# Eight experts in one loop with a question in each trip, or in one of two separate loops

## The reference, cut to what matters

```python
def moe_ffn(u, w_router, w13, w2):
    t = u.reshape(-1, D)
    logits = (t @ w_router).astype(jnp.float32)
    top_val, top_idx = lax.top_k(logits, TOP_K)          # 2 of 8
    top_w = jax.nn.softmax(top_val, axis=-1)
    out = jnp.zeros_like(t)
    for e in range(N_EXPERTS):                           # 8
        gate_e = jnp.sum(jnp.where(top_idx == e, top_w, 0.0), axis=-1)
        out = out + gate_e[:, None] * swiglu(t, w13[e], w2[e])
```

## Time and profile before

| | |
|---|---|
| median of three runs | 3160.2 us |
| profiled execution | 3152.14 us |
| its span | 3150.1 us |
| TensorE matmul busy | 2947.8 us (94%) |
| VectorE busy | 1586.7 us (50%) |
| ScalarE busy | 600.4 us (19%) |
| mean granted TensorE clock | 0.976 |
| moved | 734.33 MB, mean 233 GB/s |

### The profile page before, as it was taken

The page is one execution under the profiler, slowest core; times in us unless marked ns, Lnnn a source line. Parts: engine busy times, 40 slices in busy tenths (PEclk is TensorE's granted clock), DMA queues, the critical chain, the costliest instruction groups (busy, mean ns, idle before and its releaser), DMA issues.

```text
span 3150.1 us, 67796 instructions
## 1 busy us (share of the span) xinstructions
PE 2947.8 (94%) x28798; PEld 2597.1 (82%) x28799; DVE 1586.7 (50%) x3012; ACT 600.4 (19%) x1431; POOL 15.6 (0%) x27
## 2 busy tenths in 40 slices
PE   5999999999999999999999899988989888988988
PEld 4999888899999988899998689877856755865765
DVE  6776662476676676156765578895311101111112
ACT  1112113111211212211112111252310110110111
POOL 0000000000000000000000000000000000000000
PEclk8999999999999999999999999998999999999999
DMA  7665653456465665345555278513869768867963
GB/s 307 241 255 214 250 219 146 156 192 251 173 262 223 228 260 213 122 161 219 232 205 191 107 279 327 238 38 135 324 269 363 303 264 327 327 268 289 363 265 122
DMA packets 55615, 734.33 MB, mean 233 GB/s; under 512 B 6609, under 2 KB 6793, under 8 KB 10805
## 3 DMA queue, kind: packets, MB, share of 16 engines
q1 hardware_dynamic: 51364, 716.68, 58.4%
q0 software_dynamic: 3984, 13.74, 1.3%
HBM read 729.31 MB, written 4.23 MB: 233 GB/s over the span
## 4 chain that ended last, share of the span: by engine, by line
PE 86%; DVE 5%; DMA 5%; issue 4%; ACT 1%; SPq 0%; DVEq 0%; ACTq 0%
PE psum L746 34%; PE psum L837 17%; PE psum L1332 14%; PE psum L1376 10%; PE psum L824 3%; PE psum L740 2%; DMA ring<-in_up_dram 1%; DMA ring<-in_w_ccch_dram 1%; PE psum L1357 1%; PE psum L1392 1%; DVE ring L1883 1%; DMA ring<-in_ada_dram 1%; DMA ring<-in_m_out_dram 1%; PE psum L939 1%; DVE work L1869 1%
## 5 line engine op out<-in xcount | busy, mean ns | idle before, releaser
L746 PE MATMUL psum<-work,ring 128*128 128x128 f32 x3680 | 440.8, 275 | 2.2 <-ACT work L1465 2.2
L746 PEld LDWEIGHTS psum<-work,ring 128*128 128x128 f32 x3680 | 425.2, 192 | 3.1 <-issue 1.6
L746 PE MATMUL psum<-work 128*128 128x128 f32 x3328 | 388.8, 275 | 1.3 <-issue 1.0
L746 PEld LDWEIGHTS psum<-work 128*128 128x128 f32 x3328 | 380.0, 192 | 1.7 <-issue 1.1
L1883 DVE SCALAR_TENSOR_TENSOR ring<-ring,cond 128x1024 f32<-128x1024 f32 x240 | 279.3, 1219 | 84.4 <-DMA ring<-in_ada_dram 84.3
L837 PE MATMUL psum<-work,ring 128*128 128x256 f32 x1344 | 294.6, 381 | 6.2 <-DMA ring<-in_m_out_dram 4.3
L837 PEld LDWEIGHTS psum<-work,ring 128*128 128x128 f32 x1344 | 256.2, 191 | 43.1 <-DMA ring<-in_m_out_dram 5.1
L837 PE MATMUL psum<-h_t,ring 128*128 128x256 f32 x1280 | 278.9, 380 | 1.0 <-ACT h_t L1586 1.0
L837 PEld LDWEIGHTS psum<-h_t,ring 128*128 128x128 f32 x1280 | 242.3, 190 | 36.2 <-issue 3.1
L746 PE MATMUL psum<-h_t,ring 128*128 128x128 f32 x2272 | 266.4, 275 | 3.7 <-DMA ring<-in_up_dram 3.1
L746 PEld LDWEIGHTS psum<-h_t,ring 128*128 128x128 f32 x2272 | 259.9, 192 | 6.3 <-DMA ring<-in_up_dram 4.2
(11 more groups left out here) (382 smaller groups left out, 2930.0 us busy)
## 6 DMA issues: line engine op xcount, KB each, us to landing
ring<-in_ada_dram SPq DMA_DIRECT2D x60, 2048.0 KB, 8.1
ring<-in_up_dram SPq DMA_DIRECT2D x55, 2048.0 KB, 8.8
ring<-in_up_e_dram SPq DMA_DIRECT2D x32, 2048.0 KB, 8.7
work<-in_up_e_dram SPq DMA_DIRECT2D x32, 2048.0 KB, 7.9
ring<-in_down_dram SPq DMA_DIRECT2D x20, 2816.0 KB, 10.5
ring<-in_down_e_dram SPq DMA_DIRECT2D x16, 1792.0 KB, 9.4
work<-in_down_e_dram SPq DMA_DIRECT2D x16, 1792.0 KB, 10.2
ring<-in_w_qk_dram SPq DMA_DIRECT2D x12, 2048.0 KB, 8.2
```

What stands on the lines that cost most here:

```text
L746: mm = pe.matmul(bank(bank_of)[:, pair * P:(pair + 1) * P], w, right(i), start=(first and pair == 0 and i == 0), stop=(pair == lin.pairs - ...
```

## The change: two loops, one question, and a mark at two loop heads

The question is asked once, of the longest list. VectorE writes the maximum of the eight sums to `count`, which has one element now. TensorE reads it ahead of the loops and runs either a loop of eight short forms or a loop of eight general forms. The layer loop and the loop of short forms are opened by `hinted_loop`, which passes `hint_back_edge=True`: a marking instruction that names the loop's backward branch is put first in each trip. The inner loop over two rounds and the loop of general forms are not marked. The number of weight slots and everything else is as before.

```diff
+def hinted_loop(eng, times):
+
+    return eng.bass.Fori(0, times, engines=bass.OrderedEngineSet([eng.engine]), hint_back_edge=True)
...
-        count = sb("count", [1, NE], I32)
+        count = sb("count", [1, 1], I32)
...
-            with pe.Fori(0, DEPTH) as l:
+            with hinted_loop(pe, DEPTH) as l:
...
-            with pe.Fori(0, NE) as e:
-                many = pe.value_load(count[0:1, bass.ds(e, 1)], min_val=0, max_val=S)
-                with pe.If(many <= NARROW):
+            longest = pe.value_load(count[0:1, 0:1], min_val=0, max_val=S)
+            with pe.If(longest <= NARROW):
+                with hinted_loop(pe, NE) as e:
                     expert(e, NARROW)
-                with pe.Else():
+            with pe.Else():
+                with pe.Fori(0, NE) as e:
                     expert(e, S)
...
-            dve.tensor_copy(count[:, :], psum[0:1, 5 * 512 + S:5 * 512 + S + NE]).then_inc(dve_done, steps.one())
+            dve.reduce_max(count[:, :], psum[0:1, 5 * 512 + S:5 * 512 + S + NE], AX).then_inc(dve_done, steps.one())
```

## The result

The changed kernel took a median of 3044.82 us (four runs, 3042.27 to 3047.15) beside 3157.94 us for the kernel before on the same chip (3155.48 to 3161.18). The ratio is 0.9641 with a 95% interval of 0.9624 to 0.9658: 113 us less. The profiled execution took 3047.15 us, its span 3045.1.

The account below looks back on a forecast made before the run. TensorE, busy 94%, was taken as the bound, with pauses from refetching its code between expert trips. Terms 67.5 + 11.3 + 17.8 + 3.9 - 1 = 99.5 us took 3152.1 to 3052.6, median 3061 us, range 3049 to 3070.

Parts of the forecast that it names:

- feeding would hold at a DMA share near 0.9: Expert trips of 99 us: DMA engines busy 0.91 instead of 0.80, with six slots still covering TensorE.
- the last jump would stay: Exit of the expert loop: jump over the general form still taken once, 3.3 us as before, gain 0.
- 74.5 us become 7 x 1.0: TensorE's seven pauses between expert trips, 10.64 us each, shrink to 1.0 us each: gain 67.5 us.
- 17.8 us behind the first trip go: Idle holes in the first round of up products vanish behind the first trip, since nothing is fetched again: 17.8 us.
- gates and gather at the lower clock: Start of seven expert trips: without a long pause, 1.62 us each comes back, 11.3 us in all.
- marks: Marking instructions at the loop heads: a cost of 1 us in the sum.
- Pauses of nothing: Low bound for each pause between expert trips: 0 us, as at the inner loop's branch, against 1.0 us taken.
- with the mark most of 4.0 goes: Layer (depth) loop's one taken edge on TensorE: 2.06 us hole plus 1.9 us at lower clock; 3.9 us gained.
- I take it that they stay: Expert loop body, some 1815 instructions: its eight blocks assumed to stay in place between trips; rows proved six.
- the first rival: Expert loop: edges heal but blocks are fetched anew each trip, holes of 17.8 us remain; 3078 us, chance 0.26.

Follow-up runs that it names:

- the first kernel above: Changed kernel's split into two loops with one question, but no marks on the layer or expert loop: 3094.64 us, 0.9811 of the kernel before.
- one of 2015: Changed kernel plus 200 satisfied waits at the head of each trip, a pause without branch or fetch: 3230.93 us.
- one of 2079: Changed kernel plus 264 satisfied waits a trip, nine blocks, marks kept: 3080.17 us, 0.9758 of the kernel before.
- the one of 1750: Changed kernel without the expert loop's mark and with the second half of the tokens left out of each gather: 3040.12 us.

## Why the prediction missed its range, and what of it held

**What held:** what filled the pauses (jump, backward branch, read) and that they would go; that the body would stay, all eight blocks of it; that the clock and the holes of the first round would come back with it; that feeding would hold at a DMA share near 0.9; that the last jump would stay.

**The steps that failed.** The largest is the size of the first term, "74.5 us become 7 x 1.0": I left 1.0 us of each pause for the banks of the gather, and nothing is left. It gave 67.5 us where 75.6 were measured. Next comes the step "17.8 us behind the first trip go", which took the idle time that the view lists for the whole cost of a hole; 23.4 came back. And the 3.9 us of the layer loop's edge did not come at all. The starts of the matmuls of each part give the difference of the two stretches, 112.5 us, term by term:

| term | forecast | measured |
|---|---|---|
| seven pauses | 67.5 | 75.6 |
| gates and gather at the lower clock | 11.3 | 13.3 |
| holes in up products, behind the first trip | 17.8 | 23.4 |
| first trip and last exit | 0 | 0.2 |
| layer loop's edge | 3.9 | 0 within what can be measured |
| marks | -1 | 0 |

That is 13.0 us more than the sum. Of the 16 us between 3061 and 3044.8 another 2.3 are the kernel before, whose median was 3157.9 beside the result and 3160.2 when I wrote. Pauses of nothing, the low bound that I had given, would still have made the sum 106.5 us and the time 3054.

*Pauses.* I left 1.0 us of each because VectorE is late with the scatter's banks. From the last start of the scatter to the first of the gates a transition took 10.8 to 11.3 us before and takes 0.22 now, which is the pace inside a stretch. In the kernel the gates come first and use another bank, and the gather begins with the banks that the scatter filled, and VectorE emptied, first. I should have read the order of the banks instead of the end of the whole row.

*Holes.* The listed idle time starts at the end of the last matmul, and a matmul of 88 columns is listed as 239 ns, while in an unbroken row one starts every 38 ns (53.7 us for 1408). Each hole therefore costs 0.2 us more than the idle listed before it: 18 holes of 17.8 us make 21.4, and holes too short for the list would be the rest. In the pauses the same error is 0.16 us each, 1.1 of the 8.1 us. This is a constant error of the view that I took for exact, and the low end of my range was built on it.

*Gates and gather.* I scaled from one trip (4.56 us). The seven ran from 4.4 us, with the granted clock at 0.50 for the first 3.0 (from 2451.8 us), to 5.4, at 0.50 throughout (from 2906.3); a mean over all of them was to be had.

*Layer edge.* The step "with the mark most of 4.0 goes" failed in two ways. The branch still took 2.0 us, and the 3.2 us that TensorE gained it lost again waiting for VectorE, whose own hole of 6.26 us at that edge I had not looked up. I had asked what is late next in the expert stretch, not here.

*The mark itself, and luck.* "I take it that they stay" was my assumption: the rows before proved six blocks resident, and that eight stay is shown only by the runs above. It let the sum rest on room alone, and the mark entered it only as a cost of 1 us. That 1 us no run shows: a mark is listed with 31 to 45 ns, and it added nothing that could be measured, neither between trips, where 0.22 us is left, nor on the layer loop. The runs show that with this body room alone does not do: without marks five of seven transitions lost the head. The number came near because the mark was there, not because I had seen what it does, and that is luck. The same forecast for the loops without marks would have had a gain of 96.6 us (67.5 + 11.3 + 17.8) where 61.3 were measured, 35 us too much, by the very mechanism that I had named in the first rival as "a block past the end is brought in ahead of the branch". It had a price there without the branch; with the head thrown out, the branch pays too (6.9 us in the first kernel above).

## What to carry to other kernels

A form that is never run can still cost when it stands inside a loop: here, jumping over it, and coming back, made TensorE fetch its whole trip again, 14 to 17 us out of some 113. Count the instructions of a loop body on TensorE: one of 2015 stayed in place here, one of 2079 did not. If it reaches into the eighth block of 256, mark the backward branch: unmarked, the body of 1815 paid 6.9 us in five of seven transitions, and the one of 1750, seven blocks, 0.21 us in all. If it is longer, expect holes where instructions are short: the one of 2079 had 27.6 us of them in the up products, 38 ns from one to the next, and 2.1 in the down products, 0.43 us apart. And before marking one engine's loop, look at what the other engines do at the same edge: here VectorE stood still for 6.26 us and was next in line.

## What was not expected of the hardware

- Unmarked, the loop whose body reaches into the eighth block (1815 instructions) lost its head in five of seven transitions, with nine packets a trip, to what they suggest is a look-ahead past its end. Six instructions more ahead of the last block went with seven bad transitions of seven instead of five, and 23 us, with the same work.
- Between two satisfied waits that stand alone the sequencer takes 0.107 us, twice the 0.05 us for which one is listed.
- An unmarked backward branch with two packets beside it took 6.9 us, one whose extra packet had left 7.5 us earlier 5.5, and the one of the kernel before 4.5. VectorE stood still for 6.26 us at the layer edge although its branch instruction (L382) is listed with 0.06: there the time lies behind the branch, and only the hole before the next instruction shows it.
- A mark about halves the layer loop's branch on TensorE (3.7 to 4.0 us without it, 1.6 to 2.1 with it over the runs) but does not hide it; on the expert loop, with the head in place, nothing is left to hide (0.22 us marked, 0.21 unmarked with the short body).
